# A two-layer float32 block on one core: conditioning steps moved from the state-space rounds to the merge stage's weight slots

## The reference, cut to what matters

```python
mod_l = jnp.split((jax.nn.silu(c) @ w_ada[i] + b_ada[i])[:, None, :], 6, axis=-1)
mod_c = jnp.split((jax.nn.silu(c_ctx) @ w_ada[i] + b_ada[i])[None, None, :], 6, axis=-1)
...
z, xbc, dt_raw, u, gates = jnp.split(h @ lp['w_in'], IN_SPLITS, axis=-1)
y_a, s_f, s_b = ssd_branch(z, xbc, dt_raw, lp, h0_f, h0_b)
y_p = pool_branch(u, lp, on_grid)
...
merged = g_a * (y_a @ lp['w_branch_a']) + g_p * (y_p @ lp['w_branch_b'])
```

## Time and profile before

| what | value |
|---|---|
| median of 3 runs | 2994.97 us |
| the profiled execution's own time | 2992.41 us |
| its span | 2990.6 us |
| mean granted TensorE clock | 0.978 |
| TensorE matmul busy | 2826.0 us, 94% of the span |
| VectorE, ScalarE, GpSimd busy | 52%, 34%, 9% |
| moved from memory | 532.54 MB, 178 GB/s over the span |
| chain of waits, by engine | PE 76%, DMA 9%, DVE 8%, ACT 4% |
| state-space rounds | 199.4 to 301.6 us of the span |
| u, z, mgate | 313.65 to 339.4, to 395.9, to 444.4 us |

### The profile page before, as it was taken

One profiled execution on the slowest core, in us unless ns is written; L12 is line 12 of the kernel. 1 busy time (PEld: TensorE's weight loads), 2 busy tenths in 40 slices (PEclk: granted clock), 3 DMA queues, 4 the chain that ended last, 5 costly groups with the idle time before them and its releaser, 6 DMA issues.

```text
span 2990.6 us, 40220 instructions
## 1 busy us (share of the span) xinstructions
PE 2826.0 (94%) x17198; PEld 2149.3 (72%) x17198; DVE 1553.6 (52%) x2263; ACT 1009.1 (34%) x1436; POOL 280.3 (9%) x343
## 2 busy tenths in 40 slices
PE   7989999899998899999979899999999999998998
PEld 4854899644343478888767477888788888886998
DVE  4868546411111177675594547767465433435555
ACT  4534444311111142222553333222342222435543
POOL 0027531100000000000030000000000000200000
PEclk8999999999999999999999899999999999999999
DMA  6434646699999945553311115554355523421463
GB/s 247 141 124 150 193 139 198 232 421 421 422 421 421 412 150 172 180 178 104 95 30 35 59 55 188 181 168 152 115 169 165 159 83 101 142 85 39 139 190 100
DMA packets 337405, 536.27 MB, mean 179 GB/s; under 512 B 14372, under 2 KB 291780, under 8 KB 308420
## 3 DMA queue, kind: packets, MB, share of 16 engines
q1 hardware_dynamic: 319812, 466.52, 44.4%
q0 software_dynamic: 17408, 67.11, 6.8%
HBM read 532.54 MB, written 1.05 MB: 178 GB/s over the span
## 4 chain that ended last, share of the span: by engine, by line
PE 76%; DMA 9%; DVE 8%; ACT 4%; issue 2%; POOL 0%; SPq 0%; DVEq 0%; ACTq 0%; POOLq 0%
PE ps L186 74%; DMA raw_few<-in_w_ed 3%; DMA HF<-in_w_ed 2%; DVE ar L246 2%; DMA LF<-in_w_ed 2%; DVE LR L246 1%; ACT ar L319 1%; ACT HR L319 1%; PE ps L192 1%; DMA RAW<-in_w_ed 1%; DMA ALF<-in_w_ed 1%; DVE ar L253 1%; DVE X L246 1%; DMA ALF<-in_w_ada 1%; DVE ar L256 1%
## 5 line engine op out<-in xcount | busy, mean ns | idle before, releaser
L186 PE MATMUL ps<-AH,HR 128*128 128x512 f32 (+1 forms) x2488 | 875.5, 352 | 20.9 <-DVE AL L246 12.4
L186 PE MATMUL ps<-AL,HR 128*128 128x512 f32 (+1 forms) x2488 | 865.6, 348 | 0.0
L186 PE MATMUL ps<-AH,LR 128*128 128x512 f32 (+1 forms) x2488 | 865.1, 348 | 0.0
L246 DVE TENSOR_TENSOR LR<-RAW,HR 128x2048 fp32r<-128x2048 f32 (+3 forms) x232 | 488.6, 2108 | 403.8 <-ACT HR L319 397.7
L319 ACT ACTIVATE HR<-RAW 128x2048 fp32r<-128x2048 f32 (+3 forms) x232 | 404.1, 1744 | 598.0 <-PE ps L186 567.3
L186 PEld LDWEIGHTS ps<-AH,HR 128*128 128x128 f32 x2488 | 475.5, 191 | 93.8 <-issue 13.2
L186 PEld LDWEIGHTS ps<-AH,LR 128*128 128x128 f32 x2488 | 475.3, 191 | 58.9
L186 PEld LDWEIGHTS ps<-AL,HR 128*128 128x128 f32 x2488 | 475.8, 191 | 56.2
L186 PE MATMUL ps<-ar 64*64 64x64 f32 (+11 forms) x1126 | 143.9, 336 | 43.3 <-DVE ar L246 28.0
L256 DVE SCALAR_TENSOR_TENSOR X<-ps,mod,X 128x256 f32<-128x256 f32 x152 | 67.4, 480 | 205.7 <-PE ps L186 205.7
L246 POOL TENSOR_TENSOR ar<-ar 128x384 f32<-128x384 f32 (+7 forms) x108 | 119.2, 1113 | 424.9 <-DMA ar<-in_cst 223.4
(11 more groups left out here) (245 smaller groups left out, 3797.8 us busy)
## 6 DMA issues: line engine op xcount, KB each, us to landing
RAW<-in_f1i SPq DMA_DIRECT2D x44, 1024.0 KB, 6.4
RAW<-in_f2i SPq DMA_DIRECT2D x44, 1024.0 KB, 5.1
arf1i<-in_ada_w POOLq DMA_DIRECT2D x40, 1024.0 KB, 5.6
RAW<-in_w_in SPq DMA_DIRECT2D x32, 1024.0 KB, 5.5
arf2i<-in_ada_w POOLq DMA_DIRECT2D x24, 1024.0 KB, 5.6
RAW<-in_w_ada SPq DMA_DIRECT2D x16, 1024.0 KB, 4.9
RAW<-in_w_eg SPq DMA_DIRECT2D x15, 1024.0 KB, 22.5
HF<-in_w_ed SPq DMA_DIRECT2D x15, 1024.0 KB, 24.0
```

What stands on the lines that cost most here:

```text
L186: return self.e.matmul(o, w, x, start=start, stop=stop)
L246: return self.e.tensor_tensor(o, a, b, op) if self.e else NOTHING
```

## The change

The three calls `step(q % 2)` in the rounds go, on TensorE, ScalarE and VectorE. Nothing else is edited. Since jobs are worked off wherever a step is called, the 17 chunks that the rounds no longer do are done at the next calls: those that already stand behind the weight slots of u (4), z (8) and mgate (5 of its 8). The three turnings go with them, behind u's third, z's sixth and mgate's sixth slot.

```diff
@@ -1397,7 +1397,6 @@
                 T.mm(b[:, 0:256], K.ident[rows, 32 * d + hh:32 * d + hh + 1].broadcast_to([32, 128]),
                      o.acs[rows, 256:512], True, True).then_inc(*pe("decay", x))
-        T.step(q % 2)
         if q >= LAG:
             products(n - 2 * LAG)
@@ -1449,7 +1448,6 @@
             S.wait_ge(*dve.of("diff", x))
             S.act(o.SEG[x % NB], o.SEG[x % NB], ACT.Exp).then_inc(*act("seg", x))
-        S.step(q % 2)
         if ahead.on and ahead.r == 3:
             keys(ahead.g)
@@ -1516,7 +1514,6 @@
                 V.tt(o.SEG[x % NB], o.SEG[x % NB], o.CB[x // 16 % 2][:, 0, :], MUL).then_inc(*dve("seg", x))
-        V.step(q % 2)
         if ahead.on:
             g, r = ahead.g, ahead.r
```

## The result

The changed kernel takes **3071.56 us** (median of 5 runs, 3068.63 to 3075.39) against 2994.97 us (5 runs, 2994.40 to 3001.42): ratio 1.0254, 95% interval [1.0243, 1.0266]. That is +76.6 us. The forecast was 3052 in a range of 3021 to 3070. The sign came true, and so did the mechanism in the merge stage, though it was priced too small; the rounds won less than forecast. The value is 20 us above the forecast and 1.6 us above the range.

A forecast was written before the change was run, and what follows sets the result against it. TensorE was taken to bound the merge nearly alone, with VectorE close to it in the rounds. Terms -9.6, -4.9, +3.0 and +68.4 gave +56.9 on 2992.4, 3049.3; plus 2.6 for the median, 3052 us, range 3021 to 3070.

The forecast's parts named there:

- Merge, +68.4: Merge stage (u, z, mgate): with steps holding up projection loads in the shared ring, 199.1 us against 130.75.
- In z the same slow starts hide under the 12.5: z slots: TensorE's low-clock starts add nothing to the 12.5 us forecast from one step to the next.
- Rival D: TensorE falls to 1.2 GHz and stays there through the merge: +141 in place of 68, 3125 us; chance 0.05.
- Rival E: Contention: every projection load lands as late as the second of a pair, 7.4 us; 3077 us, chance 0.08.
- Rounds, -9.6: State-space rounds: time won by moving steps out, 4.9 us in the first 26 us and 4.7 behind.
- Ahead, +3.0: Ahead of the rounds: VectorE's first merge cut moves between the two context tiles and delays the second; ends 0 and +4.
- In the first 26 us, where TensorE is never idle, 4.9 us go, and I count them whole: First stretch of the rounds: all 4.9 us of TensorE work removed there counted as time won.
- low end of -5: Rounds: smallest forecast saving, with VectorE and GpSimd late next and only the first stretch paying.
- End of the rounds, -4.9: Last rounds: without two cuts of merge weights, the first u matmul starts near 308.8 instead of 313.65 us.
- B: Loads stay hidden, so the change only moves TensorE work: 2992 us; chance 0.05.
- C: z is not coupled and runs by the u rule, 8.3 us a slot: 3021 us; chance 0.09.
- A: The main forecast: projection loads wait for steps in the shared three-slot ring; 3052 us, chance 0.73.

The follow-up runs named there:

- second pair of profiles: The unedited kernel before and the unedited changed kernel, each run once more under its own profile: 3000.76 us and 3079.88 us, one run each.
- run 4: Changed kernel plus 16 idle matmuls at the end of each z slot, to keep TensorE's clock up: 3071.17 us.
- run 2: Changed kernel with ScalarE's and VectorE's cuts of the next z slot moved behind the current slot's first tile: 3034.38 us.
- run 3: Changed kernel with VectorE's first merge cut moved behind its pair products ahead of the rounds: 3063.92 us.
- run 7: Changed kernel with both order edits, the later z cuts and VectorE's later first merge cut: 3029.28 us.
- run 8: The kernel before, unedited, once more under its own profile: 3000.76 us, one run.
- run 1: Changed kernel with the 17 merge chunks loaded into two buffers of their own, plus one early cut held back on ScalarE and VectorE: 3013.16 us.
- run 6: Changed kernel without the 17 moved steps, modulation tiles filled with the bias, one early cut held back on ScalarE and VectorE: 2991.92 us.
- run 10: Half the change: against the kernel before, 8 of the 17 steps go to the merge and 9 stay in the rounds: 3034.66 us.

## Why the prediction was right about the ring and too small in all

*Merge, +68.4: mis-sized; measured +77.8 (+80.6 in the second pair of profiles).* By stage, with the same ends as in the windows of the changed kernel (the end of a stage's last step): u 31.2 and its slow start, some 1.2, forecast; 33.4 measured. mgate 61.5 plus the slow starts there, some 3.8, forecast; 68.2 measured, of which 1.7 are three landings over 5.44, and the slow starts are longer than priced: the first, fourth and sixth slot take 7.7, 7.5 and 8.1 us from first to last matmul where the others take 6.0, and at the first none was priced. z 101.4 forecast (98.4 is counted from z's first matmul, 3.0 behind u's last step), 107.1 measured, and that is the largest miss. **The step that failed is the sentence "In z the same slow starts hide under the 12.5".** I asked whether the *projection's* matmuls, slow at first, would hide, and they do. But the step and the sums that close the loop come after the same idle time, and they are on the chain: 2.19 us instead of 1.22 in seven of eight slots, and the turning in one of them costs 2.0 instead of 1.0, together near 7.5 us (an estimate from the chain's pieces here and in run 4). That is more than the stage's miss of 5.7, because other pieces of the loop came out shorter than priced: the low half is 2.3 and not 2.5 us in most slots, the multiply 0.34 to 0.47 and not 0.7 in six of eight. Rival D, matmuls at half speed throughout, was weighed as all or nothing, at 0.05. The step runs at 1.2 GHz in seven of eight z slots, but in the slot shown the clock is back at 1.00 from 374 us, before the next projection ends, and the stage's mean is 0.81. The Trainium skill, TensorE: Matmul & The Clock Gate, section HAM oscillation, describes a kernel in which each iteration waits for a load and starts throttled; the trace agrees with that in part, since the seven steps run at 1.2 GHz, and yet the slots end at 2.4 (the second tile of each takes 3.13 us, as in run 2 at clock 1.00). The second part is the landing: 5.74 us on average over seven slots, 6.06 in the other profile, where I took 5.4. That is a third of the way to Rival E's 7.4 at most, so E as priced fell, but its direction held, with 8 x 0.30 = 2.4 to 8 x 0.62 = 5 us in z.

*Rounds, -9.6: wrong, a saving counted that was not there. Ahead, +3.0: right for the cut.* The first profiles give -6.4 and +7.4, but they differ in the clock too. The fair pair is the kernel before in its second profile and run 3, which have "ahead" at 29.1 and 29.2 with the same low clock: the rounds fall from 99.6 to 95.6, and run 7 gives 95.5. So moving the steps out, 16.9 us of TensorE's work, won 4.0 us. Behind the sixth pair of items it won 3.4, where I took 4.7 of 12.0. In the stretch before that it won 0.6 (23.2 to 22.6; 0.4 in the changed kernel). The second step that failed is therefore **"In the first 26 us, where TensorE is never idle, 4.9 us go, and I count them whole"**. An engine busy 26.0 of 26.0 at clock 0.82 did not pay in full: with the steps gone the granted clock was lower there (0.50 and 0.83 from 208 to 212 and from 212 to 216 us in run 3, 0.72 and 1.00 in run 8), and VectorE's lines hold 37% of that stretch's chain in the changed kernel. How much of the 4.9 went to either was not separated. In the changed kernel the cut ahead of the rounds takes 2.6 of the 4.0 back, and the rest is smaller than what the clock moves: over both pairs of profiles "ahead" and rounds together went from 127.6 to 127.5. The chain of the changed kernel from 233.8 to 303.6:

```profile
by line: PE ps L186 24.8%; DVE ar L253 24.8%; DVE ar L246 23.3%; POOL X L246 7.9%; POOL ar L246 7.3%; DVE LF L246 7.1%; issue 2.4%; DVE ar L256 2.2%; ACT X L319 1.6%; DVE LF L259 0.3%; DVE ar L259 0.3%
```

TensorE's share fell from 37.5% to 24.8, and the lines of VectorE and GpSimd took its place: the end that I had named, "VectorE and GpSimd late next". My low end of -5 came nearest, but for the wrong reason: it let only the first stretch pay, and it was the later one that paid. The 4.0 also meets my own sign of being wrong, rounds that shorten by under 5. The cut ahead of the rounds was placed rightly and priced rightly (2.5 and 2.6 us in runs 3 and 7 against 3.0).

*End of the rounds, -4.9: right.* -4.8 in the first pair of profiles, -3.4 in the second; the other seven profiles without steps there all have the 7.2 us of the first.

*The sum.* From both pairs of profiles: 0 ahead and in the rounds, -4.1 at their end, +79.2 in the merge, is +75; the medians say +76.6. One end of the prediction's sum is also added up wrongly: with all low ends it is -14.5 - 5.5 + 0 + 59.3 = +39, not +43. The range did not rest on it.

*The rivals.* B, the loads hidden, is refuted by the chain itself (eight loads in z, 45.5 us) and by run 1. C, z not coupled, is refuted for this change and shown to be an order away (run 2). D came true for the steps only, E in part. The mechanism on which A stood, a step in the ring holding the load of a later slot, is shown by run 1 (same work and bytes, other buffers), by run 2 (the coupling), by run 6 (no steps, no growth) and by run 10 (price by the step).

Little can be won over the kernel before by placing these steps otherwise: without them at all the time was 4.7 us shorter (run 6), some 7 if the early cut's 2.6 are added, which is an estimate. None of the versions here that does the steps beats it.

## What to carry to other kernels

Price a small job that shares a ring by the time from its release to the next usable buffer, not by its own work: here 1.0 us of TensorE work cost 4.7 us a step, because the buffer had to be loaded and cut again, 9.8 us or more, in slots of 5.8 us. That is the price in this ring of three; with two more buffers for the chunks it was (153.3 - 128.5) / 17 = 1.5 us a step, the one wait of 8 us included. When such a wait closes a loop, go round the loop and ask for every piece what its engine did just before: here the piece behind the idle time ran at the low clock, and it was on the chain. And an engine that is never idle over a stretch need not be its whole bound: here 16.9 us of its work won 4.0. When two engines are close, take work away from the sum only after asking what the other one was waiting for.

## What the runs showed of the hardware that was not expected

- The granted clock of a stretch can differ between executions of one program: 0.98 or 0.51 on average over 186 to 199 us, with the same instructions and, just before, the same waits of 1.38 and 1.47 us on TensorE, worth 4.8 us ahead of the rounds and 2.2 at their last decay. In the profile of the earlier trace rows it falls later instead, in the rounds' first stretch (0.82).
- A 1 MB load that is issued together with a second one landed after 5.22 to 7.52 us in the profiles read for this. The last seven such loads of z took 40.2 and 42.4 us in two profiles of the changed kernel and 43.1 in run 4.
- The loads of the chunks, second of each pair, took 7.8 us as median in the changed kernel and 4.9 in the kernel before (the whole program's, 16 each). From the page of the changed kernel, its DMA issues (count, KB, median us to landing):

```profile
RAW<-in_w_in SPq DMA_DIRECT2D x32, 1024.0 KB, 5.7
...
RAW<-in_w_ada SPq DMA_DIRECT2D x16, 1024.0 KB, 7.8
```
